# Heads 4 to 7 of the first mixer: the tails multiply the softplus tile in full precision instead of its high and low part

## The reference

```
z = einsum("bqhd,bkhd->bhqk", qb, kb) * scale
log_beta = log_sigmoid(z)
log_one_minus = where(mask, log_sigmoid(-z), 0.0)          # = -softplus(z)
tail = cumsum(log_one_minus, reverse) - log_one_minus
weights = where(mask, exp(log_beta + tail), 0.0)
o = einsum("bhqk,bkhd->bqhd", weights, vb)
```

## Time and profile before

| | |
|---|---|
| median of the runs | 1300.05 us (1296.83 to 1302.20) |
| profiled execution, its own time | 1301.34 us |
| its span, first to last instruction | 1299.6 us |
| mean granted TensorE clock | 0.978 |
| busy: PE, PEld, DVE, ACT, POOL | 1235.8, 1001.8, 581.5, 476.8, 527.7 us |

### The profile page before, as it was taken

One profiled execution on the slowest core, in us unless ns is written; L12 is line 12 of the kernel. 1 busy time (PEld: TensorE's weight loads), 2 busy tenths in 40 slices (PEclk: granted clock), 3 DMA queues, 4 the chain that ended last, 5 costly groups with the idle time before them and its releaser, 6 DMA issues. The chain is left out here.

```text
span 1299.6 us, 15364 instructions
## 1 busy us (share of the span) xinstructions
PE 1235.8 (95%) x5705; PEld 1001.8 (77%) x5705; DVE 581.5 (45%) x822; ACT 476.8 (37%) x682; POOL 527.7 (41%) x296
## 2 busy tenths in 40 slices
PE   7999979999999999999798978989999999999997
PEld 6877737788888888888686767777888888888886
DVE  5786963336444444000425466874364444440002
ACT  6234535424333333111335633334243333331113
POOL 3531201436444444444553224433464444344442
PEclk9999977999999999999899999999999999999999
DMA  5320100122222222222313112011333333322211
GB/s 170 128 98 33 33 33 33 51 80 97 97 97 97 97 97 97 97 97 97 97 41 98 62 36 66 33 33 34 97 97 97 97 97 97 97 97 97 97 65 65
DMA packets 84467, 104.83 MB, mean 81 GB/s; under 512 B 2011, under 2 KB 77130, under 8 KB 84426
## 3 DMA queue, kind: packets, MB, share of 16 engines
q1 hardware_dynamic: 84266, 104.01, 24.4%
q10 hardware_dynamic: 160, 0.26, 0.1%
HBM read 101.90 MB, written 2.10 MB: 80 GB/s over the span
## 5 line engine op out<-in xcount | busy, mean ns | idle before, releaser
L401 POOL TENSOR_TENSOR w_lo<-w_raw,w_hi 128x1024 fp32r<-128x1024 f32 x188 | 452.8, 2413 | 640.4 <-ACT w_hi L524 640.2
L1359 PE MATMUL ps<-h_hi,w_hi 128*128 128x512 f32 x952 | 377.3, 396 | 5.6 <-DVE h_lo L962 2.3
L1360 PE MATMUL ps<-h_lo,w_hi 128*128 128x512 f32 x952 | 372.0, 391 | 0.0
L1361 PE MATMUL ps<-h_hi,w_lo 128*128 128x512 f32 x952 | 372.0, 391 | 0.0
L524 ACT ACTIVATE w_hi<-w_raw 128x1024 fp32r<-128x1024 f32 x190 | 199.5, 1055 | 322.5 <-PE ps L1632 164.3
L1359 PEld LDWEIGHTS ps<-h_hi,w_hi 128*128 128x128 f32 x952 | 179.7, 189 | 47.8 <-issue 8.4
L1361 PEld LDWEIGHTS ps<-h_hi,w_lo 128*128 128x128 f32 x952 | 179.5, 189 | 38.0
L1360 PEld LDWEIGHTS ps<-h_lo,w_hi 128*128 128x128 f32 x952 | 179.7, 189 | 36.2 <-issue 0.5
L1091 DVE TENSOR_TENSOR xT<-xT,ps 128x512 f32<-128x512 f32 x32 | 22.0, 687 | 268.4 <-PE ps L1632 220.2
L1125 DVE TENSOR_TENSOR ps<-ps,rbs 128x512 f32<-128x512 f32 x88 | 61.5, 698 | 169.0 <-PE ps L1361 168.6
L1632 PE MATMUL ps<-a_hi,w_lo 128*128 (+1 forms) x352 | 136.9, 389 | 0.0
(11 more groups left out here) (251 smaller groups left out, 1436.8 us busy)
## 6 DMA issues: line engine op xcount, KB each, us to landing
w_raw<-in_w_up SPq DMA_DIRECT2D x33, 1024.0 KB, 5.1
w_raw<-in_w_down SPq DMA_DIRECT2D x22, 1024.0 KB, 4.8
w_raw<-in_w_in SPq DMA_DIRECT2D x21, 1024.0 KB, 5.3
w_raw<-in_w_gate SPq DMA_DIRECT2D x11, 1024.0 KB, 5.4
w_raw<-in_w_out SPq DMA_DIRECT2D x8, 1024.0 KB, 4.9
xtok<-in_x SPq DMA_DIRECT2D x4, 512.0 KB, 5.0
out_dram<-obuf SPq DMA_DIRECT2D x8, 256.0 KB, 2.9
kT<-kT ACTq DMA_DIRECT2D x2, 128.0 KB, 2.3
```

Source lines behind the costliest of these rows:

```text
L401: pool.tensor_tensor(unit_view(w_lo, at, down), unit_raw(at, down), unit_view(w_hi, at, down).bitcast(F32), ALU.subtract).then_inc(s_lo, 1)
L1359: pe.matmul(ps[:, bank, :], whi, hi, start=first, stop=False, skip_group_check=True)
L1360: pe.matmul(ps[:, bank, :], whi, lo, start=False, stop=False, skip_group_check=True)
L1361: mm = pe.matmul(ps[:, bank, :], wlo, hi, start=False, stop=last, skip_group_check=True)
```

## The change

For heads 4 to 7 (`WHOLE = 4`) VectorE stops after the add, and signals the tile itself. The tails multiply this tile with the same constants, both read as plain f32, so that one matmul stands for the two of before. Heads 0 to 3 stay as they are.

```diff
+WHOLE = 4
@@ head(h)
                 z = zl[:, h % 4, :]
                 dve.wait_ge(s_l, h + 1)
+                if h >= WHOLE:
+                    dve.scalar_tensor_tensor(z, zps(h), 0.0, z, ALU.max, ALU.add).then_inc(s_spl, 1)
+                    return
@@ tails(h)
                         o = ZOFF[b] + P * (b2 - b)
+                        if h >= WHOLE:
+                            mm = pe.matmul(zps(h)[:, o:o + ZLEN[b2]], (ntri if b2 == b else nones)[:].bitcast(F32),
+                                           zl[:, h % 4, ZOFF[b2]:ZOFF[b2] + ZLEN[b2]],
+                                           start=False, stop=False, skip_group_check=True)
+                            continue
                         for part in (sp_hi, sp_lo):
```

## The result

The changed kernel takes 1304.58 us, the median of 20 runs (1300.63 to 1306.16), against 1300.68 us for the kernel before in the same session (20 runs, 1296.83 to 1304.63). The ratio is 1.0027, 95% interval 1.0017 to 1.0037: slower by about 3.5 us, where 2.6 us of gain were forecast. That is inside the range that the forecast gave, 1295 to 1305 us, but on the other side of the kernel before.

The account below looks back on a forecast made before the run. TensorE, busy 95% of the span, was taken as the bound. Full clock throughout would win 4.0 us; a short clock fall in tails(7) costs 1.4, leaving 2.6: 1301.3 - 2.6 = 1298.7 us, range 1295 to 1305 (8 in 10).

Parts of the forecast that it names:

- VectorE's part and the stall of head 6: Cast and subtraction go, tile ready 2.4 us earlier; hidden except at head 6, whose stall shrinks from 2.70 to 0.3 us.
- The prediction's 191.06 against 189.99 us: Head 4: line 1559 on TensorE ends at 191.06, behind the low part's 189.99, so the VectorE saving there brings nothing.
- The price of a pass: Full-precision tails on TensorE: 4.4 us a head against 2.87, 1.5 us more, 6 us over four heads.
- Rival C: Tails: a full product costs what the two parts cost, no second pass; -8.4 us, 1292.9; chance 0.03.
- The clock at tails(6): With so small a stall ahead the clock stays; tails(6) takes 4.4 us instead of 5.2 at half clock.
- Rival D: The clock falls early in tails(6) despite the short stall; +7.6 us, 1308.9 at worst, 1305 nearer; chance 0.10.
- The short fall behind the sums: In tails(7), behind the one-column sums, one short clock fall costing 1.4 us; ends were nothing and 4.4 us.
- The step that failed: TensorE time gained or lost ahead of the second stage goes to the end nearly one for one.
- Rival A: Runs before keep their clock at head 6, so passes are paid unrewarded; 3.4 us slower, 1303.5; chance 0.34.
- the 7.4 us that I counted as lost in every run: Around head 6 to the mixing: what the half-clock stretch costs the kernel before in its profile.

Follow-up runs that it names:

- e4: Kernel before with full-precision tails for heads 4, 5 and 7, head 6 left as before: 1309.80 us, ratio 1.0072 to the kernel before.
- e3: Kernel before with the full-precision tails for head 6 alone: 1294.80 us, ratio 0.9961 to the kernel before.
- e5: Kernel before with three unused full-precision matmuls filling TensorE's stall ahead of tails(6): 1300.52 us, ratio 0.9986 to the kernel before.
- e7: Full precision for head 6 alone, with half the one-column sums moved behind the first mixing product: 1297.94 us, ratio 0.9973 to the kernel before.
- a2: The changed kernel again, unedited, for a second profile: 1306.21 us.
- e6: Changed kernel with half the one-column sums moved behind the first mixing product: 1301.84 us, ratio 1.0001 to the kernel before.
- g3: Changed kernel with four unused full-precision matmuls in the stall ahead of the second block's first norm: 1300.37 us, ratio 0.9997 to the kernel before.
- g4: Kernel before with four unused full-precision matmuls in the stall ahead of the second block's first norm: 1303.04 us, ratio 1.0012.
- f1: Kernel before with one unused full-precision matmul between tails(7) and the first mixing matmul: 1304.87 us, ratio 1.0023.
- g2: Kernel before with two unused full-precision matmuls between tails(7) and the first mixing matmul: 1305.68 us, ratio 1.0027.
- g1: Changed kernel with two unused full-precision matmuls between tails(7) and the first mixing matmul: 1302.86 us, ratio 1.0019 to the kernel before.
- b2: The kernel before again, unchanged, for a second profile: 1302.37 us.
- e2: Kernel before with VectorE's shorter chain for heads 4 to 7 but single-pass tails, the high part used twice: 1299.55 us, ratio 0.9988.
- e1: Changed kernel's full-precision tails, but VectorE still casts and subtracts before it signals: 1309.47 us, ratio 1.0068 to the kernel before.
- f2: Changed kernel with three unused full-precision matmuls between tails(7) and the first mixing matmul: 1307.48 us, ratio 1.0043 to the kernel before.

## Why the prediction was wrong

- **VectorE's part and the stall of head 6**: right. 2.70 us became 0.31 us, and for heads 5 and 7 the saving was hidden; e4 shows it from the other side. For head 4 that depends on the execution: where line 1559 ran at full clock (e3, e5, e7), the kernel with the low part waited 0.8 us for it ahead of tails(4), and the changed kernel, in the same case, did not. The prediction's 191.06 against 189.99 us came from a profile with line 1559 partly at half clock.
- **The price of a pass**: 4.4 us a head, measured 4.4 (205.99 to 210.43). "1.5 us more per head" was 1.6: two heads were 3.2 us longer instead of 2.8. Rival C, that the second pass isn't there, is out.
- **The clock at tails(6)** stayed, as forecast (1.00 in 206 to 208 us). Rival D is out.
- **The short fall behind the sums**, priced at 1.4 us: in the first profile tails(7) took 7.3 instead of 4.4 us, 2.9 more; in a2 it took 6.1 us, 1.7 more, near the price. With 33.18 and 31.51 against 33.6 us the tails gained 0.4 and 2.1 us where 2.6 were forecast. e6 and e7 point to the sums as the cause of the fall: with half of them moved, it is in neither profile.
- **The step that failed** is the one beneath the sum: that time which TensorE gains or loses there "goes to the end nearly one for one". Falls of the clock behind the mixing stand at nothing in the sum; the prediction names them only in brackets, as a part of D's chance. A gain or loss ahead of the mixing does reach the second block one for one (411.38, 411.33, 411.38 and 411.32 us for the dense stretch in four profiles). Then the second mixer took 303.8 and 303.9 us before and 309.1 and 309.3 after, 5.3 us more where the sum had nothing, against the 0.4 and 2.1 us won. The work in that stretch is the same; what differs is how much of it runs at half clock: 20.5 us behind its first sums in both profiles before, 30.7 and 34.1 us in the two after. g3 and g4 show that it is no cost of the full-precision products.
- **Rival A** gave the right number, 3.4 us, and half of the reason. It said that the kernel before keeps its clock at head 6 in other executions. It lost it in both of its own profiles, but f1 and g2, with the same code up to there, kept it. In the two pairs of profiles the changed kernel was 2.5 and 3.9 us longer although the kernel before had lost its clock, so that the number of A came out is in part luck. So a part of the 7.4 us that I counted as lost in every run is not lost in every run. How much of the 3.5 us comes from this, and how much from the second mixer, the runs don't settle: the profiled pairs say the mixer, the two groups of run times of f1 and g1, some 7 us apart, show that one execution differs from the next by more than all of it.

Open: what selects the short or the long second mixer. The distance from the clock's last rise to the first mixing matmul, which L used, failed: 0.3 us (before, b2) and about 0 us (f1) went with a short one, 1.3 and 1.8 (after, a2) with a long one, but e2, at 0.05 us between the two short cases, had a long one, and so had g1 at 3.1 us. A later landmark orders the profiles better: how far behind the start of the second mixer's 16 one-column sums (636.91 us in the kernel before) the granted clock first falls. For the 16 profiles without a filled stall there:

| first fall behind the start of the sums | from there to the end | profiles |
|---|---|---|
| 3.8 to 4.0 us | 662.7 to 662.9 us | before, b2, e3 again, e6, e7, f1 |
| 1.2 us | 663.4 us | e3 |
| 0.7 to 3.2 us | 666.6 to 669.7 us | after, a2, e1, e2, e4, e5, f2, g1, g2 |

Every long one has, besides, a half clock between 750 and 785 us, and no short one has. This is an ordering found afterwards, with e3 against it; no run was made to test it, so it is not shown to be the cause.

The version to use is e3: the same edit, for head 6 alone. Ten of its twelve runs lie between 1293.3 and 1295.5 us.

## What to carry to other kernels

Apply such a trade only where the waiting is: one head of four was waited for, and it alone won 5 us. The other three, with their waits almost wholly hidden, cost 1.6 us each in passes, and all the kernels that had them in full precision without other edits also got the long second mixer in their profiles. A stall that leaves TensorE at half clock is worth more than its length, but before counting that, take a second profile: the same stall was followed by the half clock in five profiles and by the full one in two. And when a kernel has a later stage full of small stalls, compare that stage's length in both traces before explaining a difference of a few us by the edit.

## What the runs showed of the hardware

- A matmul with plain f32 operands shows two records, and at 512 columns each takes about as long as two single fp32r ones: by the weight loads of tails(4) after and before, records with 512, 384 and 256 columns are 0.43, 0.32 and 0.22 us apart against 0.23, 0.18 and 0.12 us. With 128 columns both are 0.11 us apart. So a head of the mixed sizes costs 4.4 us against 2.9 us at full clock, 1.5 times as much as its high and low products and not twice.
- One-column matmuls did not hold the clock: in e5, with no idle time from before tails(6) on, it went from 1.00 in 206 to 208 us to 0.50 in 212 to 214 us, behind the sums' start at 209.25 us; and in the kernel before, already at half, it did not rise across its sums from 213.00 to 219.78 us.
- VectorE's tensor-tensor instruction for the norm's diagonal (line 951, 128 x 512) took 0.69 us at 221 us and 2.82 us at 640 us, where GpSimd's subtraction for the weights (line 401) runs beside it. Both rows are of the kernel before; no run here takes the one away, so the cause is not shown:

```profile
221.25 0.69 DVE L951 TENSOR_TENSOR diag<-ident,small 128x512 f32<-128x512 f32 x1 [1.13 <-POOL small L416]
```

```profile
640.09 5.09 POOL L401 TENSOR_TENSOR w_lo<-w_raw,w_hi 128x1024 fp32r<-128x1024 f32 x2
640.15 2.82 DVE L951 TENSOR_TENSOR diag<-ident,small 128x512 f32<-128x512 f32 x1 [1.12 <-POOL small L416]
```
